# A Strassen feed-forward stage: where VectorE folds its running sums

## What is computed

```
def squared_relu_mlp(u, w1, w2):
    return jnp.square(jax.nn.relu(u @ w1)) @ w2
# called twice, D_MODEL = 1024, D_FF = 4096, SEQ = 512:
u = squared_relu_mlp(rms_norm(h, g_ff_pre[l]), w_ff1[l], w_ff2[l])
h = h + rms_norm(u, g_ff_post[l])
```

## Time and profile before

| | us |
|---|---|
| median of 3 runs | 2382.16 |
| lowest and highest | 2378.4, 2383.66 |
| profiled execution | 2384.59 |
| its span | 2382.8 |
| TensorE busy | 2316.8 (97%) |
| VectorE busy | 1494.7 (63%) |
| GpSimd busy | 1195.2 (50%) |
| ScalarE busy | 1175.1 (49%) |

### The profile page before, as it was taken

One profiled execution on the slowest core, in us unless ns is written; L12 is line 12 of the kernel. 1 busy time (PEld: TensorE's weight loads), 2 busy tenths in 40 slices (PEclk: granted clock), 3 DMA queues, 4 the chain that ended last, 5 costly groups with the idle time before them and its releaser, 6 DMA issues.

```text
span 2382.8 us, 39157 instructions
## 1 busy us (share of the span) xinstructions
PE 2316.8 (97%) x13090; PEld 1909.1 (80%) x13090; DVE 1494.7 (63%) x2492; ACT 1175.1 (49%) x2534; POOL 1195.2 (50%) x834
## 2 busy tenths in 40 slices
PE   7999999999999999999999999998999999999997
PEld 6887787787877778778888888887766898988886
DVE  5455556555567776863444778778675414778787
ACT  5333334334655555653744644444565644544443
POOL 4434344342443334433752587876412742687874
PEclk9999999999999999999999999999999999999998
DMA  5333333332432222223432233331322432242331
GB/s 189 113 99 102 93 103 106 98 98 63 137 94 89 88 72 91 84 66 98 133 115 72 89 109 103 98 115 54 97 67 85 137 102 71 89 128 85 116 96 62
DMA packets 126409, 232.81 MB, mean 98 GB/s; under 512 B 17184, under 2 KB 17312, under 8 KB 126240
## 3 DMA queue, kind: packets, MB, share of 16 engines
q1 hardware_dynamic: 123392, 220.08, 29.6%
q10 hardware_dynamic: 2848, 10.49, 1.3%
HBM read 208.48 MB, written 2.10 MB: 88 GB/s over the span
## 4 chain that ended last, share of the span: by engine, by line
PE 40%; issue 38%; POOL 16%; DVE 2%; DMA 1%; DVEq 1%; SPq 1%; ACT 0%; POOLq 0%; ACTq 0%
PE PS L575 37%; POOL wl L535 15%; POOL w L535 2%; PE PS L643 1%; PE PS L655 1%; DMA work<-work 1%; PE PS L610 1%; SPq L475 1%; DVE work L2095 0%; DVEq L1943 0%; DVE H L2062 0%; PE PS L650 0%; POOLq L532 0%; DMA raw<-tiles_dram 0%; DVE work L2107 0%
## 5 line engine op out<-in xcount | busy, mean ns | idle before, releaser
L535 POOL TENSOR_TENSOR wl<-raw,wh 128x512 fp32r<-128x512 f32 x586 | 819.9, 1423 | 1028.8 <-ACT wh L1311 569.4
L575 PE MATMUL PS<-uh,wh 128*128 128x512 f32 (+1 forms) x2056 | 757.9, 369 | 6.9 <-ACT work L1475 3.5
L575 PE MATMUL PS<-uh,wl 128*128 128x512 f32 (+1 forms) x2056 | 741.1, 360 | 0.0
L575 PE MATMUL PS<-ul,wh 128*128 128x512 f32 (+1 forms) x2056 | 740.4, 360 | 0.0
L575 PEld LDWEIGHTS PS<-uh,wh 128*128 128x128 f32 x2056 | 388.8, 189 | 86.3 <-issue 14.0
L575 PEld LDWEIGHTS PS<-uh,wl 128*128 128x128 f32 x2056 | 388.8, 189 | 60.1
L575 PEld LDWEIGHTS PS<-ul,wh 128*128 128x128 f32 x2056 | 389.3, 189 | 54.9 <-issue 0.5
L1311 ACT ACTIVATE wh<-raw 128x512 fp32r<-128x512 f32 x396 | 230.2, 624 | 168.4 <-PE PS L575 113.8
L575 PE MATMUL PS<-wh,forms 128*128 128x512 f32 x784 | 245.2, 394 | 12.0 <-issue 12.0
L1475 ACT ACTIVATE work<-PS 128x512 f32<-128x512 f32 (+1 forms) x152 | 87.1, 573 | 327.6 <-PE PS L575 259.4
L535 POOL TENSOR_TENSOR wl<-diagonals,wh 128x512 fp32r<-128x512 f32 x128 | 187.2, 1492 | 45.6 <-ACT wh L1311 45.6
(11 more groups left out here) (269 smaller groups left out, 3455.3 us busy)
## 6 DMA issues: line engine op xcount, KB each, us to landing
raw<-tiles_dram SPq DMA_DIRECT2D x618, 256.0 KB, 2.9
diagonals<-tiles_dram SPq DMA_DIRECT2D x128, 256.0 KB, 3.1
work<-work SPq DMA_DIRECT2D x296, 64.0 KB, 2.0
gB<-post_dram ACTq DMA_DIRECT2D x8, 512.0 KB, 3.7
H<-x_dram SPq DMA_DIRECT2D x4, 512.0 KB, 6.7
H<-x_dram ACTq DMA_DIRECT2D x4, 512.0 KB, 5.7
work<-mem_dram ACTq DMA_DIRECT2D x2, 1024.0 KB, 6.5
out_dram<-H ACTq DMA_DIRECT2D x4, 512.0 KB, 2.6
```

Of the source, the lines that this page charges most:

```text
L535: nc.gpsimd.tensor_tensor(w_of(wl, slot)[:, hc], src[:, hc], w_of(wh, slot)[:, hc].bitcast(F32), ALU.subtract).then_inc(lo_ready, 1)
L575: last = nc.tensor.matmul(out, a, b, start=start and m == 0, stop=stop and m == 2, skip_group_check=goes_on)
```

## The change

The five folds move from the last Strassen block to the one before it (block 5), one behind each of takes 0 to 4. So the helper sums are folded before the last block has added to them, and what the last block's helper products contribute goes straight to the quarters: take 0 adds the product to sums 6, 4 and 5, take 1 adds to sum 4 and take 2 to sum 5. Each take of the last block has a drain ahead of its (last) addition. The four subtractions for block 7 move from behind take 5: two to behind take 2, two to behind take 3. Take 6 of the last block comes after the loop; takes 4, 5 and 6 then follow those subtractions.

```diff
                     dve.wait_ge(tile_used, b + FF_AT[f"d{f}"] + i + 1)
                     region = PS[:, REGION[i]:REGION[i] + 2, :]
+                    into = {0: (6, 4, 5), 1: (4,), 2: (5,)}.get(i, (i,)) if f == STRASSEN - 1 else (i,)
+                    for m in into[:-1]:
+                        v.tensor_tensor(sums[m], sums[m], region, ALU.add)
+                    i = into[-1]
                     if f == 0:
                         v.tensor_copy(sums[i], region).then_inc(y_evac, 1)
                     else:
+                        if f == STRASSEN - 1:
+                            step()
                         v.tensor_tensor(sums[i], sums[i], region, ALU.add).then_inc(y_evac, 1)
...
-                    last = f == STRASSEN - 1
                     for i in range(6):
                         take(f, i)
-                        if last and i == 2:
-                            fold(2, 0)
-                            fold(1, 0)
-                            fold(6, 0)
-                            fold(5, 2)
-                            fold(4, 1)
-                            step()
-                    if last:
-                        for k in range(4):
-                            dve.wait_ge(hid_hi, hi0 + 7 * STRASSEN + k + 1)
-                            v.tensor_tensor(hid_lo7[:, k, :], hidden(7)[:, k, :], hid_hi7[:, k, :].bitcast(F32),
-                                            ALU.subtract).then_inc(hid_ready, 1)
-                        take(f, 6)
-                        step()
+                        if f == STRASSEN - 2 and i < 5:
+                            fold(*((2, 0), (1, 0), (6, 0), (5, 2), (4, 1))[i])
+                        if f == STRASSEN - 1 and i in (2, 3):
+                            for k in (2 * i - 4, 2 * i - 3):
+                                dve.wait_ge(hid_hi, hi0 + 7 * STRASSEN + k + 1)
+                                v.tensor_tensor(hid_lo7[:, k, :], hidden(7)[:, k, :], hid_hi7[:, k, :].bitcast(F32),
+                                                ALU.subtract).then_inc(hid_ready, 1)
+                take(STRASSEN - 1, 6)
+                step()
```

## The result

| | before | changed |
|---|---|---|
| median, 20 runs each (us) | 2382.3 | 2385.62 |
| lowest, highest | 2378.4, 2384.59 | 2382.99, 2391.83 |
| profiled execution (its span) | 2384.59 (2382.8) | 2391.83 (2390.0) |
| ratio | | 1.0017, 95% interval 1.001 to 1.0024 |

What follows compares the result with a forecast made beforehand. TensorE was taken to wait for the last block's folds. Per stage, +0.36 us for later product 6 less 0.9 of clock gives -0.5, -1.1 in two: 2381.1 us, own range 2377.4 to 2386.9, with rivals 2368 to 2388.

Steps and rivals of the forecast that it cites:

- product 3 late by itself: Last block: product 3 waits for take 0 and starts at 2335.94 instead of 2335.12, 0.82 us late.
- product 6 later than before: Last block: product 6 waits for take 4 behind the moved subtractions and starts at 2347.38, 0.36 us later than today.
- What bounds the kernel: Last block: TensorE waits for the folds; 6.0 us idle and 2.6 us slow clock, 8.6 us per stage.
- Part 1: Block 5: moved folds make VectorE fall behind, cycle 3.39 us against 2.72 per product; TensorE 2.31 us late in all.
- F: Block 5: time of one fold on VectorE, taken as 2.15 us beside GpSimd; bounds 1.26 and 2.31.
- The lag of VectorE: Stretch after block 5: VectorE 1.65 us late against TensorE as GpSimd's backlog meets its row additions; bounds 0 and 2.7.
- The pairs: Last block: two subtractions ahead of take 3 cost 2.9 us, two ahead of take 4 cost 3.3; bounds 1.3 and 3.5.
- half a turn: First pair, last block: one subtraction waits for part of a GpSimd instruction, the other for a full one; 2.9 us together.
- The clock: Behind the last block's idle stretch: slow clock loses 1.7 us instead of 2.6, giving 0.9 back; bounds 0 and 2.6.
- (c): VectorE bounds both blocks: F 2.31, lag 2.7, each pair 3.5 us; 5.7 us slower in two stages, 2388 us; chance 0.18.
- (a): Last block: subtractions don't collide with GpSimd, pairs cost 1.3, gap gone: 2371 us; chance 0.26 including values toward the forecast.
- (b): Block 5: folds also fall into free turns, F below 1.67, no lag; all 17.2 us come back, 2365 us; chance 0.10.

Runs made afterwards that it cites:

- direct additions: Changed kernel without folds; in every block take 0 adds to sums 6, 4 and 5, take 1 to 4, take 2 to 5: 2371.91 us, ratio 0.9959 to before.

## Why the prediction was wrong

It forecast 1.1 us less and the change costs about 4. Every wait it named was there, and in the stages TensorE stalled at no other place; two terms were sized too small. By its steps, in the second stage (starts of TensorE counted from the start of its unbroken stretch, 2046.44 before and 2052.41 after):

| step | predicted | measured |
|---|---|---|
| cycle of fold and take, block 5 | 3.39 | 3.49 |
| product 4 of block 5 late | 0.97 | 249.31 - 248.29 = 1.02 |
| product 6 of block 5 late | 2.31 | 256.27 - 253.73 = 2.54 |
| VectorE's lag on the next stretch | 1.65 | 28.00 - 25.35 = 2.65 |
| take 0 of the last block | 3.67 | 3.63 |
| product 3 late by itself | 0.82 | 4.47 - 2.66 = 1.81 |
| the two pairs | 2.9 + 3.3 | 3.56 + 3.41 |
| product 6 later than before | 0.36 | 302.90 - 300.58 = 2.32 |
| idle ahead of it | 3.3 | 3.6 |
| clock given back | 0.9 | 5.50 - 4.68 = 0.8 (start of product 6 to take 6), and 0.3 behind take 6 |
| stage | -0.5 | +1.2 |

**What bounds the kernel** held: the old gap waited for take 4 behind the folds, and without folds 6.7 of its 8.6 us per stage come back.

**Part 1** held. F was 2.26 instead of 2.15, and take 0 began 0.2 us earlier, counted from the start of the stretch (2293.42 - 2052.41 = 241.01, before 2287.63 - 2046.44 = 241.19).

**The lag of VectorE** is the step that failed. From the start of up(7) to take 0 of the last block it has 28.00 us of work (2339.52 - 2311.52) where it had 25.35 (2328.24 - 2302.89): 2.65 us late, the end of the bounds I had given, not the 1.65 I took. I let the backlog of GpSimd touch one row sum. It touched both sums behind the drains (1.60 and 1.61 instead of 0.69 each): GpSimd was at work until 2318.5, 7.0 us after the start of up(7), where before it had stopped after 3.9. A low part at 2321.67 met a half too (1.61 instead of 0.69), though GpSimd had sat idle for 2.9 us by then: VectorE was late, and the half, which came at 2321.39, now fell on it. Three times 0.9 us make the lag; the smaller differences around them cancel. The experiments show where it comes from: with no folds, or with PSUM additions in their place, the stretch took 25.35 and 25.37 us.

**The pairs** were under by 0.8: the first one was priced with half a turn for its first subtraction and met a whole one. The rows before could not tell which. GpSimd works without a pause at that place in the changed kernel and in the one without folds, yet this subtraction took 1.86 us in the first and 0.69 in the second; the forecast's half turn lies between. The subtraction right behind it took a whole turn in both (1.78 and 1.79). Lag (1.0), pairs (0.8) and F (0.2) make the 2.0 us by which product 6 is later than forecast.

**The clock** was right within 0.2, from one row of another stage.

**The rivals.** (c) is the rival that came nearest: its lag (2.7) and its pairs (3.5) were what was measured, its F was not, and its clock was not as it was before. It was to decide from 2.4 us a stage above my values; lag and pairs together reached 1.8. (a) and (b) fell: no subtraction and no fold of the changed kernel was free. In (b) the bound of 1.67 for a fold is the one at which take 2 is no longer late; for take 4 the same rows give 1.57.

## What to carry to other kernels

When work is moved under another engine's work, ask first which of its inputs lie in SBUF: here a 128x1024 addition cost 2.26 us beside GpSimd with two of them and 1.22 with one in PSUM, and more such additions were cheaper than fewer of the other kind. A collision was paid three times here: by the instruction, by the engine it blocked, and in the next stretch, in which the blocked engine's backlog met work that had run freely before. And where a row shows the other engine without a pause, price the instructions that follow each other directly with a whole turn each, and give the first of them a range from free to blocked: here 0.69 to 1.86 us, by some hundredths of a us in its start.

## What the runs showed of the hardware

The granted clock behind a pause of TensorE is not a matter of the pause's length alone. Pauses of 5.9 and 6.1 us were followed by 0.50 and 0.54, one of 4.94 by 0.50, of 3.60 by 0.64, and of 2.28 (subtractions behind take 4) by 0.68 for 5.3 us. But behind one of 1.74 (no folds) it was 1.00, and so it was behind one of 2.93 (direct additions, first stage), in these windows:
```profile
1631.00:1634.40 3.40, 0.55 (x3) 0.12 (x1) 3.28 (x3) 1.15 (x2) 3.40 (x3) 1.00 0.60 188
1634.40:1640.00 5.60, 5.53 (x24) 4.62 (x25) 2.44 (x2) 1.16 (x2) 4.07 (x4) 1.00 0.20 65
```
So a pause of 2 to 3 us cost 1.7 us of slow clock in one kernel and nothing in another. What decides it, no run here tells.
